# Both heads of a pair in one order: one 128x128 transpose per pair, one transfer per job and per load of the values

## The reference

```
def step(S, inp):
    r_t, w_t, kk_t, b_t, v_t, k_t = inp
    sa = jnp.einsum("bhvk,bhk->bhv", S, kk_t)
    S = (S * w_t[:, :, None, :] - sa[..., None] * b_t[:, :, None, :]
         + v_t[..., None] * k_t[:, :, None, :])
    return S, jnp.einsum("bhvk,bhk->bhv", S, r_t)
```

## Time and profile before

| | |
|---|---|
| runs | 2344.33, 2345.43, 2350.91 us; median 2345.43 |
| the profiled execution | 2342.53 us, span 2340.7 us |
| TensorE matmuls, weight loads | 90%, 70% of the span |
| VectorE, ScalarE, GpSimd | 66%, 38%, 33% |
| DMA packets | 215530, of which 118712 under 512 B |
| mean granted TensorE clock | 0.953 of full speed |

### The profile page before, as it was taken

The page is one execution under the profiler, slowest core; times in us unless marked ns, Lnnn a source line. Parts: engine busy times, 40 slices in busy tenths (PEclk is TensorE's granted clock), DMA queues, the critical chain, the costliest instruction groups (busy, mean ns, idle before and its releaser), DMA issues. The chain is left out here.

```text
span 2340.7 us, 37504 instructions
## 1 busy us (share of the span) xinstructions
PE 2108.7 (90%) x15256; PEld 1634.0 (70%) x15256; DVE 1539.9 (66%) x1999; ACT 878.8 (38%) x1451; POOL 782.7 (33%) x461
## 2 busy tenths in 40 slices
PE   7778999954788999899999989999899999999898
PEld 1656776744777867678887767887677777776666
DVE  5876657679776555878888884156545765645654
ACT  3433434412443464633333332244523443433321
POOL 0424334310000333677777753433322111111111
PEclk9889999977898999999999999999999999999899
DMA  7554354466655441222222236343222111101522
GB/s 280 193 192 110 104 130 113 127 180 174 169 159 177 129 161 65 81 73 81 82 78 75 76 130 251 119 148 123 63 74 81 42 50 64 55 28 46 198 72 81
DMA packets 215530, 271.12 MB, mean 116 GB/s; under 512 B 118712, under 2 KB 156216, under 8 KB 211008
## 3 DMA queue, kind: packets, MB, share of 16 engines
q1 hardware_dynamic: 210752, 251.95, 34.1%
q10 hardware_dynamic: 4608, 16.78, 2.0%
HBM read 200.48 MB, written 68.19 MB: 115 GB/s over the span
## 5 line engine op out<-in xcount | busy, mean ns | idle before, releaser
L105 PE MATMUL b_ps<-h_hi,b_wpool 128*128 128x512 f32 (+1 forms) x976 | 306.9, 392 | 19.4 <-issue 7.1
L2931 PE MATMUL g_ps<-g_h_hi,w 128*128 128x512 f32 x784 | 259.0, 402 | 5.3 <-ACT g_q L3124 5.3
L3244 POOL TENSOR_TENSOR w<-raw_down,w 128x1024 fp32r<-128x1024 f32 x38 | 94.1, 2477 | 459.8 <-ACT w L3102 459.8
L105 PEld LDWEIGHTS b_ps<-h_hi,b_wpool 128*128 128x128 f32 x976 | 186.6, 197 | 69.1 <-issue 20.0
L2200 DVE SCALAR_TENSOR_TENSOR e_vars<-grid,vec,e_vars 128x1024 f32<-128x1024 f32 x168 | 216.0, 1286 | 7.4 <-ACT e_vars L1947 4.2
L105 PE MATMUL b_ps<-h_lo,b_wpool 128*128 128x512 f32 (+1 forms) x488 | 187.4, 384 | 0.0
L2931 PEld LDWEIGHTS g_ps<-g_h_hi,w 128*128 128x128 f32 x784 | 148.4, 189 | 39.6 <-ACT g_q L3124 6.0
L2931 PE MATMUL g_ps<-g_h_lo,w 128*128 128x512 f32 x392 | 155.1, 396 | 0.0
L2612 POOL TENSOR_TENSOR g_down_lo<-raw_down,g_down_hi 128x1408 fp32r<-128x1408 f32 x26 | 86.7, 3339 | 142.1 <-ACT g_down_hi L2512 142.1
L718 POOL TENSOR_TENSOR b_wpool<-raw_in,b_wpool 128x1024 fp32r<-128x1024 f32 x26 | 67.2, 2585 | 186.5 <-ACT b_wpool L516 186.5
L2451 PE MATMUL g_pb<-g_z_hi,g_down_hi 128*128 128x512 f32 x286 | 115.2, 403 | 14.8 <-DVE g_down_lo L2689 9.8
(11 more groups left out here) (508 smaller groups left out, 5441.9 us busy)
## 6 DMA issues: line engine op xcount, KB each, us to landing
e_raw_up<-w_ffn SPq DMA_DIRECT2D x22, 1024.0 KB, 4.9
raw_down<-w_down SPq DMA_DIRECT2D x32, 704.0 KB, 4.1
c_op<-ops SPq DMA_DIRECT2D x40, 512.0 KB, 4.9
raw_down<-w SPq DMA_DIRECT2D x38, 512.0 KB, 3.6
b_xin<-ada_rows ACTq DMA_DIRECT2D x32, 512.0 KB, 5.2
raw_in<-w SPq DMA_DIRECT2D x26, 512.0 KB, 4.0
zs<-e_z SPq DMA_DIRECT2D x21, 512.0 KB, 2.6
b_ada_in<-ada SPq DMA_DIRECT2D x8, 1024.0 KB, 9.9
```

Source lines behind the costliest of these rows:

```text
L105: last = nc.tensor.matmul(out, w[:, k, :], x[:, k, cols], start=(k == 0 and n == 0), stop=(k == nk - 1 and n == 2))
L2931: mm = nc.tensor.matmul(out_bank, ww[w % 2][:, k], xx[g][:, k], start=(k == 0 and a == 0), stop=(k == KD - 1 and a == 2))
L3244: nc.gpsimd.tensor_tensor(w_lo[w % 2], raw[:, w % 2], w_hi[w % 2].bitcast(F32), ALU.subtract).then_inc(sem("lo"), 1)
```

## The change

- The second head is stored in the same order as the first, R, KK, B, K, so `store_job` is one transfer of 128 rows; the waits on its semaphore count 16 for 80.
- In the scan `token_major` turns B and K of both heads of a pair at once, a 128x128 transpose: B of both heads comes to rows 0 to 63 (`OF_B`), K of both to rows 64 to 127 (`OF_K`). There are four transposes per direction for eight, in one bank for two, and one copy of 512 columns for two of 256.
- The values of both heads go to rows 64 to 127 in one transfer (2 transfers per load for 3; the wait counts 32 for 48).
- `chain_g_values` reads rows 64 to 127 for both heads, `level_y` and its operand `td` the 32 rows of one place in rows 0 to 63 for both. Their results still go to different columns.
- `chain_z` still reads each head's own rows, but writes both heads' results to rows 0 to 63, head 0 into bank 2, head 1 into bank 3, from which ScalarE copies them.
- Masks and operand places are the same for both heads.

```diff
-                half0, half1, at = slice(0, HEAD), slice(HEAD, P), slice(s0, s0 + n // C)
-                sp.dma_start(d["ops"][x, at, half0, m].rearrange("s p z -> p s z"),
-                             ops[half0, j % 2, 0:n // C].rearrange("p s a c -> p s (a c)")).then_inc(sem(f"ops_stored{j % 2}"), 16)
-                for a in range(4):
-                    sp.dma_start(d["ops"][x, at, half1, m, C * (3 - a):C * (4 - a)].rearrange("s p c -> p s c"),
-                                 ops[half1, j % 2, 0:n // C, a]).then_inc(sem(f"ops_stored{j % 2}"), 16)
+                sp.dma_start(d["ops"][x, s0:s0 + n // C, :, m].rearrange("s p z -> p s z"),
+                             ops[:, j % 2, 0:n // C].rearrange("p s a c -> p s (a c)")).then_inc(sem(f"ops_stored{j % 2}"), 16)
...
-        bk = ring("bk", [P, 2, PAIRS, C], 2)
+        bk = ring("bk", [P, PAIRS, 2, C], 2)
...
+        z_out = lambda x, h: half(bank[x][2 + h], 1)
...
+        OF_B, OF_K = ROWS
...
-                for h in HEADS:
-                    sp.dma_start(vz[x][u % 3][ROWS[1 - h], h], d["vts"][slot, ROWS[h]]).then_inc(S(f"loaded{u % 3}_", x), 16)
+                sp.dma_start(vz[x][u % 3][OF_K], d["vts"][slot].rearrange("(h p) q v -> p h (q v)", h=2)).then_inc(S(f"loaded{u % 3}_", x), 16)
...
-                        sp.dma_start(td[x][i % 2][quarter(h, x), :, :, cols32(x)].rearrange("p j q c -> p (j q) c"),
+                        sp.dma_start(td[x][i % 2][quarter(0, x), :, :, cols32(h)].rearrange("p j q c -> p (j q) c"),
...
-            def stacked(x, u, h, q):
-
-                return op_ring[x][u % 3][ROWS[h], q, (2 * C, 0)[h]:(4 * C, 2 * C)[h]]
-
             def token_major(x, u):
-                wait(f"loaded{u % 3}_", x, (u // 3 + 1) * 48)
+                wait(f"loaded{u % 3}_", x, (u // 3 + 1) * 32)
                 wait("lm", x, 2 * u)
                 wait("yd", x, u)
+                out = bank[x][0][:].rearrange("p (q c) -> p q c", q=PAIRS)
                 for q in range(PAIRS):
-                    for h in HEADS:
-                        mm = nc.tensor.transpose(half(bank[x][h])[:, q], stacked(x, u, h, q), t["c_ident"][ROWS[h], ROWS[h]])
+                    mm = nc.tensor.transpose(out[:, q], op_ring[x][u % 3][:, q, B * C:(K + 1) * C], t["c_ident"])
                 mm.then_inc(S("p_bk", x), 1)
 
             def triangles(x, u):
                 wait("bk", x, u + 1)
                 for q in range(PAIRS):
-                    for h in HEADS:
-                        mm = nc.tensor.matmul(quad(bank[x][h])[:, q], stacked(x, u, h, q), op[x][u % 3][ROWS[h], at_of(h, (R, KK)[h]):at_of(h, (R, KK)[h]) + 2, q], start=True, stop=True)
+                    for h, rows in enumerate(ROWS):
+                        mm = nc.tensor.matmul(quad(bank[x][h])[:, q], op_ring[x][u % 3][rows, q, B * C:(K + 1) * C], op[x][u % 3][rows, R:B, q],
+                                              start=True, stop=True)
...
-                                              lm[x][u % 2][quarter(h, x), h, q, 1 ^ h, cols32(1 - x)],
-                                              td[x][u // 2 % 2][quarter(h, x), j, q, cols32(x)], start=True, stop=True)
+                                              lm[x][u % 2][quarter(0, x), h, q, 1, cols32(1 - x)],
+                                              td[x][u // 2 % 2][quarter(0, x), j, q, cols32(h)], start=True, stop=True)
...
-                    for h in HEADS:
-                        other = ROWS[1 - h]
-                        mm = nc.tensor.matmul(half(bank[x][2])[ROWS[h], q], lm[x][s % 2][other, h, q, 1 ^ h], vz[x][s % 3][other, h, q],
+                    for h, rows in enumerate(ROWS):
+                        mm = nc.tensor.matmul(half(bank[x][2])[rows, q], lm[x][s % 2][OF_K, h, q, 1], vz[x][s % 3][OF_K, h, q],
...
-                heads(half(bank[x][2], 1), (ud[x][s // 2 % 2][:, place(x, s)], gg[x])).then_inc(S("p_z", x), 1)
+                for q in range(PAIRS):
+                    for h, rows in enumerate(ROWS):
+                        mm = nc.tensor.matmul(z_out(x, h)[OF_B, q], ud[x][s // 2 % 2][rows, place(x, s), q], gg[x][rows, q], start=True, stop=True)
+                mm.then_inc(S("p_z", x), 1)
...
-                        mm = nc.tensor.matmul(half(bank[x][2])[ROWS[h], q], bk[x][s % 2][:, h, q], vz[x][s % 3][:, h, q], start=True, stop=True)
+                    for h, rows in enumerate(ROWS):
+                        mm = nc.tensor.matmul(half(bank[x][2])[rows, q], bk[x][s % 2][:, q, h], vz[x][s % 3][:, h, q], start=True, stop=True)
...
-                for h in HEADS:
-                    a = copy(bk[x][u % 2][:, h], half(bank[x][h]))
-                a.then_inc(S("bk", x), 1)
+                copy(bk[x][u % 2][:].rearrange("p q h c -> p (q h c)"), bank[x][0][:]).then_inc(S("bk", x), 1)
...
-                    a = copy(vz[x][s % 3][ROWS[h], h], half(bank[x][2], 1)[ROWS[h]], -1.0)
+                    a = copy(vz[x][s % 3][OF_B, h], z_out(x, h)[OF_B], -1.0)
```

More of the change, by code:

```diff
@@ L428, in scan_blocks @@
                             rows = slice(HEAD * h, HEAD * (h + 1))
-                            mm = nc.tensor.matmul(out[rows, j, q], src[rows, j, q, still ^ h], src[rows, j, q, moving ^ h], start=True, stop=True)
+                            mm = nc.tensor.matmul(out[rows, j, q], src[rows, j, q, still], src[rows, j, q, moving], start=True, stop=True)
                 mm.then_inc(sem(f"p_blocks{x}"), 1)
@@ L1018, in scan @@
     R, KK, B, K = range(4)
-    at_of = lambda h, a: (a, 3 - a)[h]
     with ExitStack() as st:
@@ L1200, in blocks @@
                 for j in range(2):
-                    for q in range(PAIRS):
-                        for h, rows in enumerate(ROWS):
-                            mm = nc.tensor.matmul(out[rows, j, q], src[rows, still ^ h, j, q], src[rows, moving ^ h, j, q], start=True, stop=True)
+                    mm = heads(out[:, j], (src[:, still, j], src[:, moving, j]))
                 mm.then_inc(S("p_pre", x), 1)
-            def stacked(x, u, h, q):
-                return op_ring[x][u % 3][ROWS[h], q, (2 * C, 0)[h]:(4 * C, 2 * C)[h]]
             def token_major(x, u):
-                wait(f"loaded{u % 3}_", x, (u // 3 + 1) * 48)
+                wait(f"loaded{u % 3}_", x, (u // 3 + 1) * 32)
                 wait("lm", x, 2 * u)
                 wait("yd", x, u)
+                out = bank[x][0][:].rearrange("p (q c) -> p q c", q=PAIRS)
                 for q in range(PAIRS):
-                    for h in HEADS:
-                        mm = nc.tensor.transpose(half(bank[x][h])[:, q], stacked(x, u, h, q), t["c_ident"][ROWS[h], ROWS[h]])
+                    mm = nc.tensor.transpose(out[:, q], op_ring[x][u % 3][:, q, B * C:(K + 1) * C], t["c_ident"])
                 mm.then_inc(S("p_bk", x), 1)
@@ L1261, in chain_g_state @@
                 for q in range(PAIRS):
-                    for h, rows in enumerate(ROWS):
-                        mm = nc.tensor.matmul(half(bank[x][2])[rows, q], op[x][s % 3][rows, at_of(h, KK), q], sc[x][s % 2][rows, q],
+                    for rows in ROWS:
+                        mm = nc.tensor.matmul(half(bank[x][2])[rows, q], op[x][s % 3][rows, KK, q], sc[x][s % 2][rows, q],
                                               start=False, stop=(q == PAIRS - 1))
@@ L1282, in chain_y @@
                 for q in range(PAIRS):
+                    for rows in ROWS:
+                        nc.tensor.matmul(out[rows, q], sc[x][s % 2][rows, q], op[x][s % 3][rows, R, q], start=(q == 0), stop=False)
+                for q in range(PAIRS):
                     for h, rows in enumerate(ROWS):
-                        nc.tensor.matmul(out[rows, q], sc[x][s % 2][rows, q], op[x][s % 3][rows, at_of(h, R), q], start=(q == 0), stop=False)
-                for q in range(PAIRS):
-                    for h in HEADS:
-                        mm = nc.tensor.matmul(out[ROWS[h], q], vz[x][s % 3][:, h, q], lm[x][s % 2][:, h, q, h], start=False,
-                                              stop=(q == PAIRS - 1))
+                        mm = nc.tensor.matmul(out[rows, q], vz[x][s % 3][:, h, q], lm[x][s % 2][:, h, q, 0], start=False, stop=(q == PAIRS - 1))
                 mm.then_inc(S("p_y", x), 1)
```

9 lines of the change are left out of this document (4 added, 5 removed).

## The result

The kernel after takes 2328.58 us in the median of 4 runs (2324.82 to 2330.55); the kernel before, beside it, 2348.03 (2344.33 to 2350.91). The ratio is 0.9916, 95% interval 0.9893 to 0.9939; two repeats gave 0.991 (0.9888 to 0.9931) and 0.9925 (0.9907 to 0.9943). The profiled executions differ by less, 2342.53 against 2330.55, since the one of before was faster than all four of its timed runs and the one of after was the slowest of its four.

The account below looks back on a forecast made before the run. TensorE paces the scan's last stretch, SyncE's queue the earlier late value loads and two places in the projections. Terms −3.6 − 1.1 − 3.0 + 3.1 = −4.6 us, from median 2345.43 to 2340.8 (profiled run 2337.9); range 2331 to 2351.

Parts of the forecast that it names:

- The step that failed: Job store: one transfer saves 4.1 us of SyncE issue each time, but data take 5.1 us, before 4.6.
- Low-rank weights: TensorE's three waits for these loads behind a job's store: taken as 0; bounds a gain of 1.9 each, a loss of 0.5.
- the scan's third stall: TensorE's 2.98 us wait before the transposes; Rival 2 has it shorten so the 0.94 clock does not fall, 1.4 us more.
- End of the projections: Last stores in SyncE's queue: the scan's first load starts 3.6 us sooner; bounds 0 and 5.6.
- First iteration: Weight load at the projections' start goes out 2.7 us sooner, giving TensorE 1.1 us; bounds 0 and 2.7.
- Values: Scan's value loads, one transfer for two: 3.0 us saved over three stalls; bounds 0 and 6.6.
- Transposes: Scan's eight 128x128 transposes for sixteen smaller: +0.30 us per step, +3.1 us in all where TensorE sets the pace.
- ScalarE's copies: Scan: one 512-column copy for two of 256, covered by other work: 0; uncovered 0.1 us a step.
- Row halves shared or not: Scan's values, inverse and level products on one row half: 0; bound a doubling of L1254's 1.08 us.
- Rival 3: Scan tiles sharing a row half no longer run side by side: +8.4 us in sum, 2354; chance 0.12.
- rival 1: Job stores: 1 KB packets from 128 partitions reach 345 GB/s, helping end and low-rank waits: −12.3 us, 2333; chance 0.18.
- Rival 2: SyncE sets more of the scan's stalls: −9.6 us, 2336; sign L1216's waits under 15 us; chance 0.17.

Follow-up runs that it names:

- e5: Kernel before with the next pair's low-rank weights loaded ahead of the store of job 4 instead of behind it; ratio to before 0.9994.
- e8: Kernel after with the values of the two heads loaded in two transfers, as before the change; ratio to before 0.9912.
- e6: Kernel after with each head's keys transposed by themselves (64 rows, two banks) and copied in two copies; ratio to before 0.9915.
- e3: Kernel after with each job stored in two transfers of 64 rows, both with 1 KB packets; ratio to before 0.9979.
- e11: Kernel after with each job stored in four transfers of 32 rows, all with 1 KB packets; ratio to before 0.997.
- e4: Kernel after with each job stored in four transfers, one per operand, of all 128 rows and 256-byte packets; ratio to before 0.9952.
- e7: Kernel after with head 1's z made on partitions 64 to 127 in the bank of head 0's and copied from there; ratio to before 0.9937.

## Why the prediction was wrong

- **The step that failed** is "now 1024 packets of 1 KB are 5.1 us at the same rate. So a store lands about when it did". The rate of 202 packets a microsecond was read off a transfer of 64 partitions that found the queue empty and carried over to one of 128, which ran at 374. The packets take 2.7 us, not 5.1. The trace of the kernel before held a warning: the first half of job 5, the same transfer, moved 379 packets in a microsecond at 220.25.
- **Low-rank weights, "taken as 0"**: 14.1 us in three pairs, nearly all of the miss. Even the bound (1.9 each) was too small, for two reasons. The first wait fell by 3.4 us, of which the packets' time explains 5.1 − 2.7 = 2.4 (the bound had reckoned with 345 GB/s) and the rest is open; and behind each wait the clock had been at half speed for part of 8 us: 6.1 of the 14.1 us are slower work, not idle time. The prediction gave the clock a price at the scan's third stall, but none here. And the sentence named one load behind job 4; the weight tile of r behind it counts too (e5), through ScalarE.
- **End of the projections**: −3.6 forecast, −5.5 measured, beside the bound of 5.6 for a fast store.
- **First iteration**: −1.1 forecast, −1.4 measured.
- **Values**: the stalls shrink as said and more (23.4 to 15.9 us; 21.4 with two loads), but e8 finds no time in it.
- **Transposes**: +0.30 a step forecast, +0.38 measured by the rows, and e6 finds no time in that either. In sum the scan's two terms were +0.1 us, and eleven profiles against four say +0.4: right in sum, by luck more than by the reasoning, since neither term shows in the time.
- **ScalarE's copies** were given 0 for those of bk; that those of z would overlap from one row range (1.56 us to 1.19 for a step's four) was not seen. A step without a stall is no longer for its longer transposes: 11.26 us in three steps of the kernel after, 11.44, 11.35 and 11.26 in the last three of the kernel before; the shorter wait for z fits that.
- **Row halves shared or not**: L1244 at 1.15 us for 32. Rival 3 is out.
- **Rivals**: rival 1 came about, with a price of −12.3 where some −21 came in the projections (−19 in the time). Its argument against, the same packet at 207 GB/s, rested on a store of 64 partitions onto an empty queue. Its title holds only for such stores: in job 5, behind two loads, 64 partitions are as fast. Rival 2's sign, waits before L1216 under 15 us in total, just failed (15.9), and its gain did not come.

## What to carry to other kernels

A DMA's rate is copied from a row only if the row has the same number and range of partitions and the same place in the queue (first in an empty queue, or behind others); a store of 1 MB in two halves of the rows, issued onto an empty queue, took some 4.7 us here, one of all rows 2.8. A wait of the bounding engine is priced with the slow clock behind it, and everything that stands behind a large store in the same queue is listed, down to the load at which another engine's in-order queue stops: moving one of those loads alone may gain nothing. What is saved in a stretch whose pace another resource sets can come back as a wait.

## What the runs showed of the hardware

- Stores of 1 KB packets that find the queue empty: 202 GB/s from rows 0 to 63 (e3), 200 from two strips of 32 of them (e11), 383 from all 128 in one transfer (kernel after). Job 5's, behind two loads: 382 from rows 0 to 63 (before), 376 to 380 from both halves (e3), 382 from strips of 32 (e11).
- 256-byte packets: 290 GB/s from all 128 rows (e4), 286 from rows 64 to 127 of job 5 (before, at 222 us).
- A wait of 4.1 us of TensorE is followed by 8 us at a mean granted clock of 0.74; one of 0.7 us by none (1.00).
- ScalarE's 64x256 copies overlap when they read the same 64 rows (75 of 372 ns in 22.3 us) and do not when the rows alternate (76 of 379 ns in 28.8 us, e7).
- The scan of one and the same kernel took 319.2, 323.5 and 326.0 us in three profiles, its projections 324.6 to 326.4.
